# Regrouping gate jobs, gate loads and one mix in a hybrid trunk step on one core

## The chip, the cores and the metric

The kernel runs on one core of one Trainium2 chip. The metric is the time of one execution on the device in microseconds (us); for a kernel it is the median of its runs.

## The reference

The program is one inference step of a trunk with two layers (`DEPTH = 2`) on 384 tokens of width 1024: 128 context tokens and 256 tokens of a denoising step. A layer mixes tokens in four parallel branches, which share one input projection, and then applies a mixture of 16 experts. The gates of the branches come from the same projection; the change touches their computation and the differential attention.

```python
h = rms_norm(x, p['norm1_w']) * (1 + scale1) + shift1
(mq, mk, mv, mo, mg, nq, nk, nv, dq, dk, dv, sz, sxbc, sdt, gpre) = split_cols(h @ p['w_in'])
...
br = jnp.stack([a_out, b_out, c_out, d_out], axis=2)
gates = jax.nn.sigmoid(gpre.reshape(B, S, N_BRANCH, D_MODEL))
mixed = jnp.sum(gates * jnp.einsum('bsnc,ncd->bsnd', br, p['w_branch']), axis=2)
x = x + gate1 * (mixed @ p['w_out'])
h2 = rms_norm(x, p['norm2_w']) * (1 + scale2) + shift2
x = x + gate2 * expert_choice_ffn(h2, p['w_router'], p['w_gate'], p['w_up'], p['w_down'])
```

The branches are an mLSTM and an SSD scan (each in both directions), a neighbourhood attention and a differential attention, where `a = p[0] - lam * p[1]` mixes two softmaxes before the product with the values.

## The kernel before

Each engine has its own instruction list, written out by hand, and the lists meet by semaphores. In a layer's mixing stage TensorE does, in this order: the input projection (L887 to L905), the neighbourhood attention (L1001), the differential attention (L1062), the scans (L1104 to L1191), a tail of jobs (L1193), the transposes of the branch outputs (L1200), the branch products (L1209), the output products (L1223). Then comes the expert stage (L1246 to L1409), whose weights are streamed from HBM into seven slots.

**Jobs.** The 4096 gate columns of `w_in` are cut into 32 gate jobs (`g0` to `g31`), 24 matmuls of 128x384 each: three passes of split weights over eight blocks of rows. Eight parts (`p`) and sums (`s`) of the modulation weights `w_ada` make 16 more. Their order is the table `JOB_SITES` (L118): every entry is a place in TensorE's list where `job()` (L916) is called, with the jobs done there. ScalarE takes each job's bank in the same order with `take_job()` (L1553): two banks serve in turn, so a job waits until the job two before it is taken. Gates 0 to 23 are stored to HBM as they are taken (L1571; the issue comes with the next take); gates 24 to 31 stay in `GATES`.

**Splits.** Before a quarter of a weight tile is used, ScalarE copies its rounded part into one of four buffers (`high_parts`, L1470) and GpSimd subtracts it (`low_parts`, L709, L717). `AHEAD` (L243) says up to which quarter ScalarE splits after each job; a quarter can be split when its tile has landed and the job four before it is done. `high_parts` waits for the landing of a tile when it comes to the tile's first quarter. The branch weights are two tiles of 2 MB and their first quarter waits for both (L548).

**Loads.** SyncE issues the tile loads in the order of `JOB_TILES` (L139, loop L635), each after the job that frees its slot: a tile of gates after the last gate of the tile two before, an ada tile after the part before. Then it issues the two branch tiles (L645), waiting first for gate 27 and then for part 7, and after all jobs the saved x and the first half of `w_out` (L648 to L650).

**Differential attention.** VectorE finds the maxima of a unit (`df_max`), mixes the two softmaxes (`df_mix`, L2054) and takes the product of an earlier unit out of its bank (`df_take`, L2064). The loop is at L2069. TensorE's `df_turn(u)` (L1042) waits for mix u, `df_out(u)` (L1052) for the take of unit u-1.

**Scans.** For each of the two scans VectorE turns eight decay rows into exponents, and multiplies them with TensorE's scores (`decays`, L2088). TensorE does four jobs among the first rows, one behind the last rows, two behind the last scores (L1126, L1127), two ahead of the state products (L1144), and in the second scan one, two and three (L1160 to L1171). ScalarE's takes are placed to match (L1643 to L1666).

**From the tail to the branch products.** VectorE's norms end with `br_ready` (L2234). TensorE waits for it, transposes the outputs into six banks and does the last job. ScalarE copies the six banks (L1667), takes the last job, and issues the first four gate loads (L1674 to L1681): 576 KB each, two of them into the room of the scan's work tiles once `br_ready` is there, two into room that VectorE's `tokens_free` (L2254) gives free. VectorE makes the low part of each bank behind ScalarE's copy (L2245), then waits for the stores of the states and sets `tokens_free`. Each branch product (eight, L1209) is 24 matmuls; VectorE gates it (L2256 to L2267) with a loaded gate tile; the third product and each later one waits for the gating of the one two before.

Of the kernel before, what the change touches and what calls it, by code (L numbers as in the profile page):

```python
# [70 lines left out]
def constants():  # L71
# [31 lines left out]
    for g in range(4):  # L103
        for r in range(2):
# [19 lines left out]
JOB_ORDER = tuple(_s[1] for _s in JOB_SITES)  # L124
NA_JOBS = [len(_s[1].split()) for _s in JOB_SITES if _s[0] == "na"]
DF_JOBS = [len(_s[1].split()) for _s in JOB_SITES if _s[0] == "df"]
# [120 lines left out]
SPILLED = 24  # L247
# [16 lines left out]
def trunk_program(nc, dr, outs):  # L264

    (y_prompt, y_sample, new_na_k, new_na_v, new_diff_k, new_diff_v, new_C, new_n, new_m, new_ssm) = outs
    with ExitStack() as ctx:
# [3 lines left out]
        sem = {n: ctx.enter_context(nc.semaphore(n)) for n in SEMS}  # L271
# [5 lines left out]
        spilled = [ctx.enter_context(nc.semaphore(f"spilled{i}")) for i in range(8)]  # L277
# [16 lines left out]
        def rounded(v):  # L294
            return bass.AP(as_fp32r[v.tensor.name], v.offset, v.ap)
# [469 lines left out]
        def _(pe):  # L765
# [62 lines left out]
            for l in range(L):  # L828
# [87 lines left out]
                def job():  # L916

                    j = jobs[0]
                    jobs[0] += 1
                    kind, i = JOBS[j]  # L920
                    if j >= 2:
                        pe.wait_ge(sem["job_evac"], NJ * l + j - 1)
                    else:
                        pe.wait_ge(sem["proj_evac"], N_PROJ * l + (19, N_PROJ)[j])
                    if kind == "sum":
                        pe.wait_ge(sem["job_evac"], NJ * l + JOBS.index(("part", i)) + 1)
                        mm = ada_sum(job_bank(j), MPL(i))
                    elif kind == "part":
                        mm = ada_partial(job_bank(j), tile(("mix", l, 7 + [t_[:2] for t_ in JOB_TILES].index(("ada", i)))))
                    else:  # L930
                        hi, lo_ = next_quarter()[0]
                        for k in range(KC):
                            mm = three_passes(PS[:, job_bank(j), 0:T], (hi[:, k, :], lo_[:, k, :]), h_in(k), k == 0, k == KC - 1)
                    mm.then_inc(sem["job_out"], 1)
# [189 lines left out]
                pe.wait_ge(sem["pm_ready"], 16 * l + 6)  # L1124
                scores(0, 3)
                job()  # L1126
                job()  # L1127

                pe.wait_ge(sem["pm_ready"], 16 * l + 8)
                for i, (t, d, b, bq) in enumerate(((0, 0, 2, None), (0, 1, 3, None), (1, 0, 4, 5), (1, 1, 6, 7), (2, 0, 2, 3), (2, 1, 4, 5))):  # L1130
# [30 lines left out]
                decay_row(1, 4)  # L1161
                decay_row(1, 5)
                job()
                job()
                decay_row(1, 6)
                decay_row(1, 7)
                pe.wait_ge(sem["pm_ready"], 16 * l + 12)
# [22 lines left out]
                        mm = pe.matmul(PS[0:64, 5, 64 * c:64 * c + 64], KW[:, d, h, :], BTM[:, 64 * (h // 2):64 * (h // 2) + 64], start=True, stop=True)  # L1190
                mm.then_inc(sem["st_out"], 1)  # L1191

                for _ in range(6):  # L1193
                    job()


# [222 lines left out]
        def _(act):  # L1419
            def copy(dst, src, scale=1.0):  # L1420
                return act.activation(dst, src, ACT.Copy, scale=scale)  # L1421
# [45 lines left out]
            for l in range(L):  # L1467
# [175 lines left out]
                for c in range(8):  # L1643
                    decayed(0, c)
                    if c >= 2:
                        take_job()
                take_job()

                act.activation(W1[:, 0:768].rearrange("p (a b) -> p a b", a=TT), MO[:, :, :], ACT.Tanh, scale=0.5)
                act.activation(W1[:, 768:1536].rearrange("p (a b) -> p a b", a=TT), SZ[:, :, :], ACT.Tanh, scale=0.5).then_inc(sem["tanh_out"], 1)  # L1650
# [4 lines left out]
                    copy(CN_OUT[0:64, d, :, :], PS[0:64, 7 if d == 0 else 2, 0:260].rearrange("p (a b) -> p a b", a=4)).then_inc(sem["st_evac"], 1)  # L1655
                for c in range(8):
                    decayed(1, c)
                    if 2 <= c <= 4:
                        take_job()
                take_job()  # L1660
                take_job()
                take_job()
                act.wait_ge(sem["st_out"], 2 * l + 2)
                copy(SS_OUT[0:64, :, :], PS[0:64, 5, :].rearrange("p (a b) -> p a b", a=8)).then_inc(sem["st_evac"], 1)
                for _ in range(6):
                    take_job()  # L1666
                for g in range(6):  # L1667
                    t, half = g // 2, g % 2
                    act.wait_ge(sem["brt_out"], 6 * l + g + 1)
                    copy(rounded(BRT[:, 4 * half:4 * half + 4, t * 128:(t + 1) * 128]), PS[:, 2 + g, :].rearrange("p (a b) -> p a b", a=4)).then_inc(sem["brt_evac"], 1)  # L1670
                take_job()


                for slot in spilled:  # L1674
                    act.wait_ge(slot, 16 * (SPILLED // 8) * (l + 1))
                for dc in range(4):
                    if dc == 0:
                        act.wait_ge(sem["br_ready"], l + 1)
                    if dc == 2:
                        act.wait_ge(sem["tokens_free"], l + 1)  # L1680
                    act.dma_start(GT[dc % 4], spill[l, dc]).then_inc(gate_in[dc % 4], 16)  # L1681
                for dc in range(8):
                    high_parts(Q_BRANCH + dc + 5)
                    act.wait_ge(sem["bp_evac"], 8 * l + dc + 1)
# [91 lines left out]
        def _(dve):  # L1776
# [34 lines left out]
            for l in range(L):  # L1811
# [233 lines left out]
                def df_max(u):  # L2045
                    dve.wait_ge(sem["ds_out"], 12 * l + u + 1)
                    if u >= 2:
                        dve.wait_ge(sem["dpt_out"], 12 * l + u - 1)
                    i, w = u % 2, (128 if u < 4 else 384)
                    dve.tensor_reduce(SMX[:, i, :], PS[:, 2 + 2 * i:4 + 2 * i, 0:w], AX.X, ALU.max, negate=True).then_inc(dve_step, 1)  # L2050
                    dve.wait_ge(dve_step, step())
                    TS(DMX[:, i, :], SMX[:, i, :], 32 ** -0.5, None, ALU.mult).then_inc(sem["d_max"], 1)
# [13 lines left out]
                    t, h = u // 4, u % 4  # L2066
                    dve.tensor_copy(DQK[:, t, h * 64:h * 64 + 64], PS[:, 7, 0:64]).then_inc(sem["do_evac"], 1)

                for i in range(15):  # L2069
                    if i < 12:  # L2070
                        df_max(i)
                    if i >= 3:
                        df_take(i - 3)
                    if 1 <= i <= 12:
                        df_mix(i - 1)

                def head_norm(src, n, c, scale, eps, power, lo):

# [326 lines left out]
```

## Time and profile before

| | |
|---|---|
| median of 3 runs | 1991.64 us (1990.75 to 1997.35) |
| the profiled execution's own time | 1997.49 us |
| its span in the profile | 1995.7 us |
| TensorE matmuls busy | 1786.2 us (90%) |
| VectorE busy | 632.3 us (32%) |
| ScalarE busy | 556.9 us (28%) |
| GpSimd busy | 513.6 us (26%) |
| mean granted clock of TensorE | 0.98 |
| DMA | 567.78 MB, mean 285 GB/s |

PE is TensorE, PEld its weight loads, DVE VectorE, ACT ScalarE, POOL GpSimd, SP SyncE; a q behind a name is that engine's DMA issue. A time is counted from the start of the span. Busy time says how long an engine had instructions running; the chain of the profile says which of them set the end. Layer 0's mixing stage lies at about 60 to 500 us and layer 1's at 1035 to 1480 us; the expert stages, with the DMA engines nearly full, lie behind each.

### The profile page before, as it was taken

The page shows a single profiled execution, that of the slowest core. Times are in us where ns is not written, and L with a number is a line of the kernel's source. Part 1 is how long each engine was busy: PE and PEld are TensorE (multiplying, and loading weights), DVE is VectorE, ACT ScalarE, POOL GpSimd, SP SyncE. Part 2 cuts the span into 40 slices and gives each one's busy share as a digit, 9 for nine tenths or more (in the row PEclk, how much of TensorE's full clock was granted, in tenths as well). Part 3 has the DMA queues.
Part 4 walks back from the last instruction along what each step waited for, and adds up shares of the span by engine and source line. Part 5 has one row for each costly group of instructions (what it writes and reads, how often), then busy time and mean ns, then how long its engine had stood idle before and what let it go on. Part 6 is the DMA issues. An engine that isn't in the chain of part 4 may idle for free.

```text
span 1995.7 us, 22783 instructions
## 1 busy us (share of the span) xinstructions
PE 1786.2 (90%) x9208; PEld 1138.6 (57%) x9208; DVE 632.3 (32%) x1363; ACT 556.9 (28%) x1070; POOL 513.6 (26%) x654
## 2 busy tenths in 40 slices
PE   6999999979899888888889999998999988888787
PEld 3788997879443222222258889887975322222223
DVE  1287344764400000101144853548622000000011
ACT  3444344223421101111144444432333111011011
POOL 0787344246100000000037754424631000000000
PEclk8999999989999999999999999899999999999999
DMA  9535534465799999999973354353465999999996
GB/s 349 126 104 182 192 117 156 130 231 193 297 376 426 427 425 428 427 427 427 426 211 127 106 204 154 109 189 132 169 253 211 404 428 426 426 428 427 427 426 260
DMA packets 123544, 567.78 MB, mean 285 GB/s; under 512 B 21808, under 2 KB 31280, under 8 KB 98352
## 3 DMA queue, kind: packets, MB, share of 16 engines
q1 hardware_dynamic: 112656, 543.91, 68.9%
q10 hardware_dynamic: 9920, 20.84, 2.8%
q0 software_dynamic: 864, 1.58, 0.3%
q8 instruction: 73, 1.20, 0.2%
q14 instruction: 31, 0.25, 0.0%
HBM read 550.57 MB, written 15.73 MB: 284 GB/s over the span
## 4 chain that ended last, share of the span: by engine, by line
PE 54%; DMA 36%; DVE 6%; ACT 2%; SPq 1%; issue 1%; POOL 0%; ACTq 0%; DVEq 0%
PE banks L776 29%; PE banks L1322 11%; DMA work<-in_w_gate 7%; DMA ring<-in_w_up 6%; DMA work<-in_w_up 6%; DMA ring<-in_w_down 6%; DMA ring<-in_w_gate 4%; DMA work<-in_w_down 3%; PE banks L782 2%; DMA ring<-in_w_ada 1%; PE banks L1082 1%; PE banks L1292 1%; PE banks L788 1%; ACT work L1421 1%; DMA work<-gates_spill 1%; ACT hT L1450 1%
## 5 line engine op out<-in xcount | busy, mean ns | idle before, releaser
L717 POOL TENSOR_TENSOR ring_fp32r<-ring,ring_fp32r 128x256 fp32r<-128x256 f32 x592 | 461.3, 812 | 854.9 <-ACT ring_fp32r L1421 854.2
L1322 PE MATMUL banks<-ring,work 128*64 128x512 f32 x1776 | 402.7, 597 | 77.0 <-DMA ring<-in_w_gate 33.5
L776 PE MATMUL banks<-xT_fp32r,ring_fp32r 128*128 128x384 f32 x1280 | 349.9, 346 | 1.8 <-POOL ring_fp32r L717 1.8
L1421 ACT ACTIVATE work<-banks 32x512 f32<-32x512 f32 (+7 forms) x404 | 205.4, 529 | 454.4 <-PE banks L1322 250.8
L1322 PEld LDWEIGHTS banks<-ring,work 128*64 128x64 f32 x1776 | 122.5, 136 | 335.4 <-issue 199.0
L1322 PE MATMUL banks<-work 128*64 128x512 f32 x972 | 225.8, 601 | 40.4 <-DMA work<-in_w_gate 14.9
L776 PEld LDWEIGHTS banks<-xT_fp32r,ring_fp32r 128*128 128x128 f32 x1280 | 237.2, 191 | 14.7 <-issue 7.2
L776 PE MATMUL banks<-hT_fp32r,ring_fp32r 128*128 128x384 f32 x640 | 217.3, 340 | 0.0
L2317 DVE SCALAR_TENSOR_TENSOR xT<-banks,mod,xT 128x128 f32<-128x128 f32 (+1 forms) x128 | 47.1, 413 | 445.5 <-PE banks L1358 445.1
L1421 ACT ACTIVATE ring_fp32r<-ring 128x1024 fp32r<-128x1024 f32 (+1 forms) x164 | 154.5, 969 | 94.1 <-PE banks L776 74.2
L1322 PEld LDWEIGHTS banks<-work 128*64 128x64 f32 x972 | 67.5, 137 | 180.7 <-issue 112.5
L1727 ACT ACTIVATE work<-banks 128x512 f32<-128x512 f32 x32 | 19.1, 597 | 483.5 <-PE banks L1322 483.5
L776 PE MATMUL banks<-work_fp32r,ring_fp32r 128*128 128x384 f32 x768 | 142.7, 346 | 8.3 <-DVE work L2267 8.3
L776 PEld LDWEIGHTS banks<-work_fp32r,ring_fp32r 128*128 128x128 f32 x768 | 137.5, 192 | 11.6 <-DVE work L2267 8.9
L776 PE MATMUL banks<-ring_fp32r,xT_fp32r 128*128 128x512 f32 (+1 forms) x480 | 136.2, 369 | 1.2 <-DVE small L1857 1.2
L776 PEld LDWEIGHTS banks<-hT_fp32r,ring_fp32r 128*128 128x128 f32 x640 | 122.6, 192 | 1.3 <-issue 0.3
L2339 DVE TENSOR_TENSOR work<-work,banks 128x512 f32<-128x512 f32 x32 | 22.0, 688 | 292.3 <-PE banks L1322 292.2
L776 PEld LDWEIGHTS banks<-ring_fp32r,xT_fp32r 128*128 128x128 f32 x480 | 86.7, 189 | 16.1 <-DVE small L1857 1.4
L1322 PE MATMUL banks<-hT,work 128*64 128x512 f32 x324 | 75.2, 599 | 20.7 <-DMA work<-in_w_gate 8.2
L776 PE MATMUL banks<-ring_fp32r,hT_fp32r 128*128 128x512 f32 (+1 forms) x240 | 88.4, 368 | 0.0
L1566 ACT ACTIVATE work<-banks 128x384 f32<-128x384 f32 x64 | 31.3, 489 | 163.0 <-PE banks L776 163.0
L2336 DVE SCALAR_TENSOR_TENSOR work<-work,banks 128x512 f32<-128x512 f32 x32 | 21.8, 681 | 124.8 <-ACT work L1421 67.9
(293 smaller groups left out, 1736.1 us busy)
## 6 DMA issues: line engine op xcount, KB each, us to landing
ring<-in_w_up SPq DMA_DIRECT2D x38, 2048.0 KB, 30.6
ring<-in_w_gate SPq DMA_DIRECT2D x37, 2048.0 KB, 30.6
ring<-in_w_down SPq DMA_DIRECT2D x36, 2048.0 KB, 30.1
ring<-in_w_in SPq DMA_DIRECT2D x28, 2048.0 KB, 8.3
ring<-in_w_ada SPq DMA_DIRECT2D x24, 2048.0 KB, 8.4
work<-in_w_down SPq DMA_DIRECT2D x20, 2048.0 KB, 30.6
work<-in_w_gate SPq DMA_DIRECT2D x18, 2048.0 KB, 30.6
work<-in_w_up SPq DMA_DIRECT2D x16, 2048.0 KB, 30.6
```

Of the source, the lines that this page charges most:

```text
L717: ins = pool.tensor_tensor(rounded(w_), w_, rounded(hi_), ALU.subtract)
L776: mm = pe.matmul(dst, a_, b_, start=(first and i == 0), stop=(last and i == 2))
L782: mm = pe.matmul(PS[32 * g:32 * g + 32, bank, :], c32[:, k, :], w[:, k, :], start=(k < 4), stop=(k >= 4), tile_position=(0, 32 * g))
L788: mm = pe.matmul(PS[:, bank, 2 * j:2 * j + 2], partial[:, j // 2, 128 * (j % 2):128 * (j % 2) + 128], K("adasel"), start=True, stop=True)
L1082: pe.matmul(PS[:, 4 + c % 4, 0:T], ident[:, r:r + 1].broadcast_to([128, 128]), ROWS[:, 0, :], start=True, stop=True)\
L1292: mm = pe.matmul(dst, rounded(strided(part[:, t, 512 * (q // 8):512 * (q // 8) + 512], q // 2 % 4)), rounded(SEL[:, t, a:b, :].rearrange(" ...
L1322: mm = pe.matmul(dst[64 * hf:64 * hf + 64, :], x(k), w[kk][:, 512 * hf:512 * hf + 512], start=(k == 0), stop=(k == KC - 1), tile_position= ...
L1421: return act.activation(dst, src, ACT.Copy, scale=scale)
L1566: ins = act.activation(GATES[:, i % 8, :], PS[:, job_bank(j), 0:T], ACT.Tanh, scale=0.5)
L2317: ins = STT(xT[:, dc, a:b], PS[:, bank, a:b], mod[:, 40 + dc, g:g + 1], xT[:, dc, a:b], ALU.mult, ALU.add)
L2336: STT(SA, TH, 1.0, PS[:, 2 * (e % 2), :], ALU.add, ALU.mult).then_inc(dve_step, 1)
L2339: TTo(HH[:, e % 2, :], SA, PS[:, 2 * (e % 2) + 1, :], ALU.mult).then_inc(sem["hh_ready"], 1)
```

## The change

Gate 23 and those behind it move later in the job order: the scans have two gate jobs less and the tail has eight jobs in place of six, with part 7 ahead of gate 27. ScalarE's takes follow. ScalarE issues the first two gate loads ahead of its copies of the branch banks and the next two ahead of its take of the last job. VectorE does the last differential mix ahead of the takes of units 9, 10 and 11.

```diff
-             ("scan0", "g20"), ("scan0", "p3"), ("scan0", "g21 s3"), ("scan0", "g22"), ("scan0", "p4 g23"),
-             ("state0", "s4 p5"), ("scan1", "g24"), ("scan1", "s5 g25"), ("state1", "p6 g26 s6"), ("tail", "g27 p7 g28 s7 g29 g30"), ("branch", "g31"))
+             ("scan0", "g20"), ("scan0", "p3"), ("scan0", "g21 s3"), ("scan0", "g22"), ("scan0", "p4"),
+             ("state0", "s4 p5"), ("scan1", "g23"), ("scan1", "s5"), ("state1", "p6 g24 s6"), ("tail", "g25 p7 g26 s7 g27 g28 g29 g30"), ("branch", "g31"))
...
                 scores(0, 3)
                 job()
-                job()
...
                 decay_row(1, 5)
                 job()
-                job()
                 decay_row(1, 6)
...
-                for _ in range(6):
+                for _ in range(8):
                     job()
...
                     if c >= 2:
                         take_job()
-                take_job()
...
-                    if 2 <= c <= 4:
+                    if 2 <= c <= 3:
                         take_job()
...
-                for _ in range(6):
+                for _ in range(8):
                     take_job()
+                for slot in spilled:
+                    act.wait_ge(slot, 16 * (SPILLED // 8) * (l + 1))
+                act.wait_ge(sem["br_ready"], l + 1)
+                for dc in range(2):
+                    act.dma_start(GT[dc], spill[l, dc]).then_inc(gate_in[dc], 16)
                 for g in range(6):
                     t, half = g // 2, g % 2
                     act.wait_ge(sem["brt_out"], 6 * l + g + 1)
                     copy(rounded(BRT[:, 4 * half:4 * half + 4, t * 128:(t + 1) * 128]), PS[:, 2 + g, :].rearrange("p (a b) -> p a b", a=4)).then_inc(sem["brt_evac"], 1)
+                act.wait_ge(sem["tokens_free"], l + 1)
+                for dc in range(2, 4):
+                    act.dma_start(GT[dc], spill[l, dc]).then_inc(gate_in[dc], 16)
                 take_job()
-                for slot in spilled:
-                    act.wait_ge(slot, 16 * (SPILLED // 8) * (l + 1))
-                for dc in range(4):
-                    if dc == 0:
-                        act.wait_ge(sem["br_ready"], l + 1)
-                    if dc == 2:
-                        act.wait_ge(sem["tokens_free"], l + 1)
-                    act.dma_start(GT[dc % 4], spill[l, dc]).then_inc(gate_in[dc % 4], 16)
...
-                for i in range(15):
-                    if i < 12:
-                        df_max(i)
+                for i in range(12):
+                    df_max(i)
                     if i >= 3:
                         df_take(i - 3)
-                    if 1 <= i <= 12:
+                    if i >= 1:
                         df_mix(i - 1)
+                df_mix(11)
+                for i in range(9, 12):
+                    df_take(i)
```

## Rows read from the trace of the kernel before

**Rows 1.** The page's costliest groups of instructions.

```profile
L1322 PE MATMUL banks<-ring,work 128*64 128x512 f32 x1776 | 402.7, 597 | 77.0 <-DMA ring<-in_w_gate 33.5
```

**Rows 2.** Chain that ended last, in order of time, layer 0.

```profile
340.83 4.36 PE banks L776 x24
...
368.56 4.30 PE banks L776 x24
372.86 1.29 PE banks L1082 x4
...
415.57 1.38 DVE work L2234
...
427.12 9.20 DMA work<-gates_spill
```

**Rows 3.** TensorE in order of time: start us, us, what [idle before <-releaser].

```profile
308.90 0.55 PE L1049 MATMUL banks<-cst,work 128*128 128x128 f32 x3 [2.15 <-DVE work L2062]
...
391.71 0.44 PE L776 MATMUL banks<-xT_fp32r,ring_fp32r 128*128 128x384 f32 x1
...
416.99 5.38 PE L1204 MATMUL banks<-cst,work 128*128 128x128 f32 x24 [5.38 <-DVE work L2234]
...
440.03 39.53 PE L776 MATMUL banks<-work_fp32r,ring_fp32r 128*128 128x384 f32 x216 [4.82 <-DVE work L2267]
...
1284.64 0.55 PE L1049 MATMUL banks<-cst,work 128*128 128x128 f32 x3 [2.16 <-DVE work L2062]
...
1370.48 0.44 PE L776 MATMUL banks<-xT_fp32r,ring_fp32r 128*128 128x384 f32 x1
...
1397.65 5.13 PE L1204 MATMUL banks<-cst,work 128*128 128x128 f32 x24 [7.27 <-DVE work L2234]
...
1418.88 21.33 PE L776 MATMUL banks<-work_fp32r,ring_fp32r 128*128 128x384 f32 x111 [3.47 <-DVE work L2267]
...
1509.70 0.36 PE L1272 MATMUL banks<-cst,work 16*128 16x16 f32 x3 [1.10 <-DVE work L2304]
```

**Rows 4.** VectorE in order of time, layer 0.

```profile
304.47 1.06 DVE L2062 SCALAR_TENSOR_TENSOR work<-work,small 128x384 f32<-128x384 f32 x1
...
340.20 0.42 DVE L2120 TENSOR_TENSOR work<-work,banks 128x256 f32<-128x256 f32 x1
...
368.91 0.41 DVE L2120 TENSOR_TENSOR work<-work,banks 128x256 f32<-128x256 f32 x1
...
384.08 1.37 DVE L2178 TENSOR_TENSOR work<-work 128x768 f32<-128x768 f32 x1
...
409.23 0.96 DVE L2229 TENSOR_TENSOR work<-work 128x768 f32<-128x768 f32 x1
```

**Rows 5.** Stretches: us, busy PE PEld DVE ACT POOL, granted clock, DMA, GB/s.

```profile
308.90:321.18 12.28, 11.96 (x57) 8.92 (x61) 5.71 (x20) 2.39 (x4) 4.63 (x7) 0.86 0.39 150
1284.64:1299.95 15.31, 14.99 (x57) 11.16 (x61) 5.71 (x20) 2.38 (x4) 4.62 (x7) 0.67 0.32 123
...
1509.70:1515.00 5.30, 5.20 (x21) 2.85 (x21) 4.00 (x7) 1.06 (x2) 0.00 (x0) 1.00 0.00 0
```

**Rows 6.** SyncE's queue in order of time, both layers.

```profile
396.18 2.25 SPq L563 DMA_DIRECT2D ring<-in_w_branch  x2
...
1374.94 2.25 SPq L563 DMA_DIRECT2D ring<-in_w_branch  x2
```

**Rows 7.** ScalarE in order of time, both layers.

```profile
414.15 2.19 ACT L1421 ACTIVATE ring_fp32r<-ring 128x512 fp32r<-128x512 f32 x4 [6.17 <-DMA ring<-in_w_branch]
...
416.61 1.14 ACT L1421 ACTIVATE ring_fp32r<-ring 128x512 fp32r<-128x512 f32 x2
...
1391.38 2.19 ACT L1421 ACTIVATE ring_fp32r<-ring 128x512 fp32r<-128x512 f32 x4 [4.64 <-DMA ring<-in_w_branch]
...
1402.22 1.20 ACT L1421 ACTIVATE work_fp32r<-banks 128x512 fp32r<-128x512 f32 x2 [0.26 <-PE banks L1204]
```

**Rows 8.** Line 563, the weight loads of 320 to 420 us.

```profile
DMA to landing us min/median/max: 7.7/9.7/16.0
```

## The prediction

> **What bounds the kernel now.** First I read, among the page's costliest groups, the expert matmuls (L1322): of the 77.0 us that TensorE stood idle before one group of them, a load of gate weights ended the largest part, 33.5 [rows 1]. The expert stages are a stream of weight loads, set off by the branch and output products at the end of each mixing stage; so a microsecond saved before that end should move the rest of the program one for one.
>
> Then I read the chain that ended last, in order of time, through layer 0's mixing stage [rows 2]. Two gate jobs lie on it inside the scans (4.36 and 4.30 us). Behind the scans it is one VectorE chain, the norms that end with br_ready at 415.57 + 1.38 = 416.95; then TensorE transposes the branches, does the last gate job, and the first branch product waits for a 9.20 us gate load before the stream of 216 matmuls starts at 440.03.
>
> Last I read TensorE's own order of time with its waits in brackets [rows 3]. TensorE is without a gap from 308.90 to the end of the tail jobs (416.99 - 5.38 = 411.61). Its waits in layer 0 are 2.15 (last differential mix), 5.38 (br_ready) and 4.82 us (gate load); in layer 1 they are 2.16, 7.27 and 3.47. That is all this change can win by filling gaps, except what the clock gives back.
>
> **The mix ahead of three takes.** VectorE ended the mix before the last at 304.47 + 1.06 = 305.53 [rows 4], and stood until TensorE came to 308.90 - 2.15 = 306.75, because a take that needs TensorE's product was ahead of the last mix; take (some 0.2) and mix then filled TensorE's wait of 2.15 [rows 3]. Without the take ahead the mix starts at 305.53 and costs 1.95 (its length as it was) to 2.8 us (GpSimd splits beside it until then, and a VectorE product is 1.37 us beside a split for 0.96 without [rows 4]). It ends at 307.5 to 308.3, and TensorE waits 0.7 to 1.6 in place of 2.15: I take 1.1, so 1.05 saved per layer. The three takes behind it come up to 1 us later, under the transposes of the last unit.
>
> **The clock behind that wait.** From the end of the wait to the end of the first scan job layer 0 takes 12.28 us at a granted clock of 0.86, layer 1 15.31 us at 0.67 [rows 5]: part of it runs at 1.2 GHz and the rest at 2.4. All at 2.4 GHz it would be about 10.5 (busy time times granted clock, plus the 0.32 idle), so 1.8 and 4.8 us hang on the clock. A wait of 1.10 elsewhere was followed by a granted clock of 1.00 [rows 3, 5], and 1.1 is what I expect here; but that is one row, in a stretch of other work. The ends are 0 and 6.6 us, and I take half, 3.3.
>
> **Two jobs out of the scans.** 4.36 + 4.30 = 8.66 us leave TensorE's gapless stretch. What would be late next is VectorE: the score products behind the first job wait for its last decay product, which ended at 340.20 + 0.42 = 340.62 against 340.83 when the removed job began, and those behind the second for 368.91 + 0.41 = 369.32 against 368.56 + 1.29 (the decay rows that stood behind the job, at 372.86) = 369.85 [rows 2, 4]. Both are just in time, so the whole 8.66 counts. The bounds are 0 (VectorE slips by as much) and 8.66.
>
> So the first tail job starts 8.66 + 1.05 = 9.7 earlier, at 382.0 for 391.71, and in layer 1 at 1360.8 for 1370.48. I count on from that start, s.
>
> **The tail.** It took 411.61 - 391.71 = 19.9 us; with two more jobs it takes 28.5. br_ready came at s + 25.2 (layer 0) and s + 27.1 (layer 1, 1397.65). GpSimd's splits now fall more into the VectorE chain. By the 0.41 that a 768-column product loses, and about three such steps under a split, two more splits in layer 0 cost some 2 us and one more in layer 1 some 1. br_ready thus comes at s + 27 to 28, hidden by the jobs. The wait for it is gone.
>
> **What is late next: the branch weights.** Their two 2 MB loads are issued in order by SyncE, the first after gate 27. That job was the first of the tail (ending at s + 4.4); now two gates, part 7 and sum 7 stand before it. Four gates, the part and the sum made the 19.9, so part and sum are 19.9 - 4 x 4.33 = 2.6, and it ends at 3 x 4.36 + 2.6 = s + 15.7; part 7's load stands behind its own. In layer 0 the first load was issued at 396.18 and ScalarE went on with the split of both at 414.15, 17.97 later; in layer 1 it was 1374.94 and 1391.38, 16.44 later [rows 6, 7]. I take the middle, 17.2: landing at s + 33 (15.8 with the issue). ScalarE waits for it right behind its take of gate 28, and behind that wait stand, in its order: the takes of gates 29 and 30, three splits, the first two gate loads, and the six copies of the turned branches. From 414.15 to the end of the third split (416.61 + 1.14) took 3.6; with both takes 4.1. The copies run 0.60 each [rows 7], 3.5 together, and VectorE's last low part ends 0.7 later. So TensorE, which has turned the branches by s + 28.5 + 5.4 = 33.9, starts the products at 33.0 + 4.1 + 3.5 + 0.7 = s + 41.3. The last gate job lies inside that stretch (it needs gate 29's take at s + 34.5).
>
> The Trainium skill, DMA: Bandwidth & Descriptors, sections Bandwidth and Latency and other measured facts, gives 425 GB/s for a large read and about 2 us of fixed cost. By that, as an estimate, 4.2 MB land 11.9 us after the issue, 5.3 sooner, and the program would take 1961. The two measured landings disagree with it, and the sum goes by them.
>
> **Gate loads ahead of the last job.** Their issue moves from 427.12 to behind br_ready and the third split, s + 37. With the 9.20 us of the row [rows 2], where two more of them were beside them, they would land at s + 46.2, and probably sooner. The first product ends at 41.3 + 4.2 = s + 45.5. So the wait shrinks to 0 to 0.7; the second product (to s + 49.7) covers VectorE's 3.6 us of gating, and the long stream starts at s + 49.7. The other two loads now wait for tokens_free ahead of the last take; that take then comes at s + 42, and TensorE wants it for the second product at s + 45.5. The waits for the spill stores are over long before (gate 23's store moves with its job and is still issued ahead of the tail). The wait for br_ready ahead of the copies costs nothing, as the transposes need it anyway.
>
> **Moved past.** On SyncE the tile of gates 28 to 31 is loaded after gate 23, behind the sixth ada tile: issued about 362, landing some 10 later, split at 373. Ada tile 5 now has 10 us instead of 14 until its job; 7.7 us was the quickest load of this stretch [rows 8], so a wait of up to 1 us is possible. GpSimd's state stores go out behind the splits of gates 29 and 31, by s + 22, some 20 ahead of tokens_free, which waits for them.
>
> **Sum.** The long stream started at 440.03 - 391.71 = s + 48.3 and at 1418.88 - 1370.48 = s + 48.4. Now it is s + 49.7 with s 9.7 earlier: 8.4 saved per layer, 16.8 in both, and 3.3 from the clock: 20.1 us. The profiled execution's own time is 1997.49 (span 1995.70), 5.9 above the median of the three runs and at their upper end; the change comes off either. Against 1991.64 that is 1971.5.
>
> **Rivals.**
> - *The branch weights are not late.* A 2 MB load by itself lands in 7.7 us [rows 8], two of them side by side thus in 7.7 to 15.4, by the middle 11.6 in place of 17.2: landing at s + 27.4, products start at s + 35.7, the gate load (s + 31.5 + 9.2) and VectorE's 3.6 put the stream at s + 44.3, 13.7 saved per layer. 1991.6 - 27.4 - 3.3 = **1961**. Against it stand both measured pairs; for it, that no other load now runs beside them.
> - *The weights come later by some microseconds*, or the idle time that is left brings 1.2 GHz into the products: 4 to 7 per layer, **1978 to 1985**.
> - *The scans do not get shorter.* The two margins are 0.21 and 0.53 us; if VectorE slips, the jobs move but nothing ends sooner: s + 49.7 against s + 48.3 with s 1.05 earlier, 0.3 lost per layer, less the clock's 3.3: **1989**, no change.
> - *Slower: the two loads land one behind the other.* If each takes the longest landing measured, 16.0 [rows 8], the second lands 32 after the issue, 14.8 later than I count: 6.4 lost per layer, 12.8 less 3.3, **2001**. It decides from a landing 25.6 us after the issue on. Against it: the pair took 16.4 and 18.0 though issued 1.9 apart.
>
> **How the numbers follow.** A measurement of this kernel can tell 0.3%, 6 us, from no change. Forecast 0.58 (its own range 1966 to 1978), weights early 0.17, weights later 0.10, scans unchanged 0.08, loads in series 0.07. The first three are faster: 0.85; same 0.08; slower 0.07. The range from 1960 to 1984 leaves out the last two and the outer ends of the second and third, 0.2 in all.
>
> **What would show it.** TensorE's wait ahead of the last differential transposes near 1 us; no job between the last decay row's scores and the numerators; the tail gapless for 28.5 us and the branch transposes without a wait; a ScalarE wait of some 12 us for in_w_branch behind gate 28; a wait of 2 to 5 us around the last gate job; no wait of VectorE for gates_spill over 1 us. I am wrong if the scans keep their length, if that ScalarE wait is gone, or if the expert stages stretch by what the mixing stages save.

## The result and the profile after

The changed kernel took 1971.29 us in the median of 4 runs (1969.93 to 1972.82) beside 1991.2 for the kernel before (4 runs): a ratio of 0.9902, 95% interval 0.9878 to 0.9926. The forecast was 1971.5. The profiled execution took 1972.1 us (span 1970.3, clock 0.988). Lines of the changed kernel stand one to three numbers lower than before (L1204 is now L1202, L1421 is L1419, L2062 is L2059), and one higher again where the stores are moved. Here and below, "1.33 for 2.15" means 1.33 where it was 2.15.

TensorE in order of time, with the waits in brackets, first layer 0 and then layer 1:

```profile
305.89 0.55 PE L1049 MATMUL banks<-cst,work 128*128 128x128 f32 x3 [1.33 <-DVE work L2059]
...
407.15 2.84 PE L1202 MATMUL banks<-cst,work 128*128 128x128 f32 x24 [0.22 <-DVE work L2233]
414.73 0.69 PE L776 MATMUL banks<-xT_fp32r,ring_fp32r 128*128 128x384 f32 x1 [4.75 <-ACT work L1564]
...
1270.73 0.55 PE L1049 MATMUL banks<-cst,work 128*128 128x128 f32 x3 [1.33 <-DVE work L2059]
...
1371.99 2.84 PE L1202 MATMUL banks<-cst,work 128*128 128x128 f32 x24 [0.22 <-DVE work L2233]
1379.66 0.45 PE L776 MATMUL banks<-xT_fp32r,ring_fp32r 128*128 128x384 f32 x1 [4.83 <-ACT work L1564]
1386.43 1.82 PE L776 MATMUL banks<-work_fp32r,ring_fp32r 128*128 128x384 f32 x9 [0.74 <-issue]
```

Beside [rows 3]: the wait for the last mix is 1.33 for 2.15; that for br_ready is 0.22 for 5.38 and 7.27; the gate-load wait (4.82 and 3.47) is gone. A new wait stands ahead of the last gate job, 4.75 and 4.83 us, put down to ScalarE's take.

The chain that ended last, in order of time, says what that take waited for:

```profile
334.33 1.85 PE banks L782 x16
336.18 2.82 PE banks L1098 x24
...
358.96 0.79 PE banks L788 x8
359.75 1.40 PE banks L1082 x4
...
378.77 4.37 PE banks L776 x24
383.14 1.85 PE banks L782 x16
...
394.89 18.20 DMA ring<-in_w_branch
414.73 53.49 PE banks L776 x288
...
1379.66 6.03 PE banks L776 x24
...
1386.43 46.51 PE banks L776 x264
```

In the scans the numerators (L1098) and the second direction's scores (L1082) now stand right behind an ada job (a part, L782, or a sum, L788); the two gate jobs that [rows 2] had there are gone. The tail starts at 378.77 for 391.71. What the last gate job waited for, by this chain, is the load of the branch weights, 18.20 us on it. ScalarE and SyncE in order of time agree:

```profile
394.47 4.00 SPq L563 DMA_DIRECT2D ring<-in_w_branch  x2
...
413.15 1.15 ACT L1419 ACTIVATE ring_fp32r<-ring 128x512 fp32r<-128x512 f32 x2 [14.02 <-DMA ring<-in_w_branch]
413.80 0.81 ACTq L1668 DMA_DIRECT2D work<-gates_spill  x2
...
417.03 3.02 ACT L1419 ACTIVATE work_fp32r<-banks 128x512 fp32r<-128x512 f32 x6
```

From the issue to the split of the weights it is 413.15 - 394.47 = 18.68 us. ScalarE stood 14.02 of them, with the takes of gates 29 and 30 behind it, and TensorE needs the first of these for its last gate job.

The stretches of [rows 5], of the same lengths from the end of the mix wait:

```profile
305.89:318.17 12.28, 11.96 (x69) 8.56 (x69) 5.79 (x21) 3.90 (x7) 5.32 (x8) 1.00 0.50 191
1270.73:1286.04 15.31, 14.99 (x81) 10.53 (x82) 7.11 (x26) 4.50 (x8) 5.31 (x8) 1.00 0.51 174
```

The granted clock behind the mix wait is 1.00 in both layers, for 0.86 and 0.67, and the same time holds 69 and 81 matmuls (the first count in brackets) for 57 and 57. The expert stream, in the page's costliest groups, has not changed, so what the mixing stages save the program saves:

```profile
L1320 PE MATMUL banks<-ring,work 128*64 128x512 f32 x1776 | 404.4, 599 | 77.9 <-DMA ring<-in_w_gate 33.3
```

**Where the time came from.** From the start of the mix wait (before 308.90 - 2.15, after 305.89 - 1.33) to the end of the branch products (before 440.03 + 39.53 by [rows 3], after 414.73 + 53.49) layer 0 takes 163.66 us for 172.81: 9.15 saved. In layer 1 the same stretch ends at 1386.43 + 46.51 for 1418.88 + 39.65 = 1458.53 and takes 163.54 for 176.05: 12.5 saved. The row of before:

```profile
1418.88 39.65 PE L776 MATMUL banks<-work_fp32r,ring_fp32r 128*128 128x384 f32 x216 [3.47 <-DVE work L2267]
```

Together 21.7; the medians differ by 19.9. The spans of the two profiled executions differ by more, 25.4 us: 2.2 of these lie ahead of the first mix wait and 1.7 between the two stretches, where the change moves nothing; they are not counted as its gain.

### The profile page after: what moved, and what is told of

Same layout as the page of the kernel before. It is cut to its first block, busy times and chain, and to the rows that moved or that the text cites. A ratio compares the mean times of both kernels' runs of the same rounds, so it can differ in the third digit from the quotient of the medians.

```text
span 1970.3 us, 22783 instructions
## 1 busy us (share of the span) xinstructions
PE 1772.6 (90%) x9208; PEld 1128.7 (57%) x9208; DVE 634.2 (32%) x1363; ACT 555.9 (28%) x1070; POOL 514.5 (26%) x654
## 4 chain that ended last, share of the span: by engine, by line
PE 56%; DMA 37%; DVE 3%; ACT 2%; SPq 1%; issue 0%; POOL 0%; ACTq 0%; DVEq 0%
PE banks L776 31%; PE banks L1320 11%; DMA work<-in_w_gate 7%; DMA work<-in_w_up 6%; DMA ring<-in_w_down 6%; DMA ring<-in_w_up 6%; DMA ring<-in_w_gate 4%; DMA work<-in_w_down 3%; PE banks L782 2%; DMA ring<-in_w_branch 2%; PE banks L1098 1%; DMA ring<-in_w_ada 1%; PE banks L1082 1%; PE banks L1290 1%; PE banks L788 1%; ACT work L1419 1%
## 5 line engine op out<-in xcount | busy, mean ns | idle before, releaser
L1419 ACT ACTIVATE work<-banks 32x512 f32<-32x512 f32 (+7 forms) x404 | 205.4, 529 | 452.4 <-PE banks L1320 253.1
L1419 ACT ACTIVATE ring_fp32r<-ring 128x1024 fp32r<-128x1024 f32 (+1 forms) x164 | 154.8, 970 | 106.9 <-PE banks L776 69.5
```

## The experiments

The theory after this reading: the three parts add up, and what the two moved jobs save in the scans is mostly eaten by the branch weights. The rival: those weights are late for a reason that an earlier issue does not change. The kernels ran in three groups, each beside its own runs of the kernel before (medians 1991.72 of 17 runs, 1995.42 of 6, 1992.79 of 10).

| kernel | median us | ratio to before | 95% interval |
|---|---|---|---|
| mix_only | 1983.06 | 0.9963 | 0.9949 to 0.9977 |
| loads_only | 1982.62 | 0.9953 | 0.9938 to 0.9969 |
| jobs_only | 1988.88 | 0.9984 | 0.9969 to 0.9999 |
| branch_split | 1958.64 | 0.9833 | 0.9818 to 0.9849 |
| branch_late | 1972.03 | 0.9883 | 0.9865 to 0.9901 |
| mix_loads | 1970.51 | 0.9876 | 0.9859 to 0.9894 |
| branch_split_p7 | 1955.11 | 0.9802 | 0.9782 to 0.9821 |
| branch_best | 1959.63 | 0.9819 | 0.9803 to 0.9835 |
| stores_early | 1965.68 | 0.9866 | 0.9841 to 0.9890 |
| p7_stores_early | 1955.28 | 0.9807 | 0.9787 to 0.9827 |
| mix_loads_stores | 1977.98 | 0.9921 | 0.9899 to 0.9942 |
| after_again | 1971.31 | 0.9890 | 0.9872 to 0.9908 |

### The three parts, each alone

**mix_only**: the kernel before with this part of the change.

```diff
-                for i in range(15):
-                    if i < 12:
-                        df_max(i)
+                for i in range(12):
+                    df_max(i)
...
+                df_mix(11)
+                for i in range(9, 12):
+                    df_take(i)
```

> Against the kernel before at 1991.2. Theory (each part is worth the TensorE wait that it closes, and the waits do not overlap): the wait ahead of the last differential transposes falls from 2.15 to 1.33 us as in the changed kernel, 1.6 us in both layers, and up to 6.6 more if the clock stays at 2.4 GHz behind it: 1983 to 1990. Rival (the mix only shifts a wait to the take behind it): 1991, with a new wait of TensorE ahead of the last unit's product.

1983.06, as expected. The two waits are 1.34 and 1.33 and the clock behind both is 1.00. The gain, 0.37% or 7.4 us (4.6 to 10.2 by its interval), is far more than the 0.82 saved per layer; the stretches of 12 to 15 us behind this wait, over all kernels of this study, put the rest down to the clock. With a wait of 2.14 or 2.15 (before, loads_only, jobs_only) the granted clock was 0.86, 0.67, 1.00, 0.67, 0.86 and 1.00; with 1.33 or 1.34 it was 1.00 in 21 of 22 (0.86 in layer 0 of branch_best).

**loads_only**: the kernel before with ScalarE's gate loads moved as in the change.

```diff
+                act.wait_ge(sem["br_ready"], l + 1)
+                for dc in range(2):
+                    act.dma_start(GT[dc], spill[l, dc]).then_inc(gate_in[dc], 16)
                 for g in range(6):
...
+                act.wait_ge(sem["tokens_free"], l + 1)
+                for dc in range(2, 4):
+                    act.dma_start(GT[dc], spill[l, dc]).then_inc(gate_in[dc], 16)
                 take_job()
```

> Against the kernel before at 1991.2. Theory: the gate loads, issued at br_ready some 9 us sooner, land before the first product ends; the waits of 4.82 and 3.47 us ahead of the third product go: 8.3 us, with up to 3 more from the clock behind them: 1980 to 1983. Rival (the loads only come into the way of the saved x and the output weights, or the take of the last job behind tokens_free is the new wait): 1989 to 1993.

1982.62, as expected. In its chain of waits the transposes still wait for br_ready (6.38 and 6.41 in TensorE's order of time), but the last gate job and all products then run without a gap:

```profile
417.64 4.91 PE banks L1204 x24
422.55 50.46 PE banks L776 x288
```

The gain, 0.47% or 9.4 us (6.2 to 12.3 by its interval), agrees with the two waits (4.82 + 3.47) and some clock behind them. Before, the 216 matmuls behind the wait took 39.53 us [rows 3]; in the changed kernel 264 take 46.51 in layer 1, so 216 would take 38.05. The wait thus had a clock price of some 1.5 us per layer behind it; the granted clock of the first 6 us behind it was 0.73 and 0.72.

**jobs_only**: the kernel before with the new `JOB_SITES`, the `job()` calls and the takes of the change.

```diff
-("scan0", "p4 g23"), ("state0", "s4 p5"), ("scan1", "g24"), ("scan1", "s5 g25"),
+("scan0", "p4"), ("state0", "s4 p5"), ("scan1", "g23"), ("scan1", "s5"),
...
-                for _ in range(6):
+                for _ in range(8):
                     job()
```

> Against the kernel before at 1991.2. Theory: the tail starts 8.7 us sooner, but the branch weights land 18.7 after gate 27 and the gate loads are issued only after the last job, so the third product starts at s + 53 in place of s + 48.3: 3.7 us saved per layer, 1984. Rival (the moved jobs are nearly the whole gain of the change): 17 us, 1974.

1988.88, a smaller gain than expected. The wait for br_ready is gone (0.23), but TensorE waits for the branch weights instead, and the gate-load wait stays:

```profile
420.23 0.69 PE L776 MATMUL banks<-xT_fp32r,ring_fp32r 128*128 128x384 f32 x1 [5.25 <-ACT work L1564]
...
440.56 9.69 PE L776 MATMUL banks<-work_fp32r,ring_fp32r 128*128 128x384 f32 x46 [4.61 <-DVE work L2264]
```

So 8.66 us leave the scans of each layer and 1.6 us of the program's time per layer are left, by an interval that nearly reaches no change. The three gains add to 1.00%, and the change has 0.98%. That the parts add up does not follow from it: mix_loads, below, breaks it.

### Are the branch weights what takes the jobs' gain?

**branch_split**: the changed kernel; SyncE loads part 7's half of the branch weights first, and no longer behind gate 27.

```diff
-for i, job in enumerate((("gate", 27), ("part", 7))):
+for i, job in ((1, ("part", 7)), (0, ("gate", 27))):
```

> The changed kernel (1971.3), with SyncE waiting for part 7 and loading its half of the branch weights first, then gate 27 and the other half. Theory (ScalarE's wait of 14.0 us for the branch weights is what holds the last gate job, TensorE's waits of 4.75 and 4.83): only one tile is left to land behind gate 27, some 8 to 11 us after it in place of 18.7, so TensorE's wait goes and the products start 4 to 5 us sooner in each layer: 1961 to 1963. Rival (the wait is hidden by the copies of the branch banks and the gate loads behind it): 1970 to 1972.

1958.64, better than expected and 12.7 below the change. The first half goes out at 386.90, and ScalarE's split, which needs both, comes at 408.99 for 413.15. The wait ahead of the last gate job is gone in both layers; what is left stands ahead of the products:

```profile
417.34 32.98 PE L776 MATMUL banks<-work_fp32r,ring_fp32r 128*128 128x384 f32 x186 [1.33 <-issue]
...
1375.69 46.52 PE L776 MATMUL banks<-work_fp32r,ring_fp32r 128*128 128x384 f32 x264 [1.00 <-issue]
```

**mix_loads**: the kernel before with both other parts, without the moved jobs (the diffs of mix_only and loads_only).

> The kernel before with the mix and the gate loads of the change, and its own job order. If the parts add up, 0.9963 x 0.9953 = 0.9916 of the kernel before, 1975, and the moved jobs are worth only some 3 to 4 us in the changed kernel. Rival (the jobs make room for the loads, so the parts need each other): 1980 or more.

1970.51: faster than both expectations, and as fast as the whole change (1971.29, and 1971.31 in the repeat; branch_late, in the same group, 1972.03). The two parts together gain 1.24% where alone they gain 0.84% in sum; the kernel before ran 3.7 us slower in this group than in the first, and how much of the difference is real stays open. The sum of three that matched the change was thus a coincidence. The transposes of mix_loads wait 5.39 and 7.29 us for br_ready, and nothing waits behind. From the start of the mix wait to the end of the branch products it takes 163.60 and 164.34 us, the change 163.66 and 163.54. So in the change as it stands the moved jobs are worth nothing that these runs can tell: they exchange the wait for br_ready for the one on the weights. Either has 1.2 GHz behind it for a part: the granted clock is 0.72 in the change's last gate job of layer 1, which takes 6.03 us (the tail's first 4.37), and 0.52 in the transposes of mix_loads in layer 0. The change first, then mix_loads:

```profile
1379.66:1385.69 6.03, 6.03 (x24) 5.71 (x24) 3.04 (x6) 5.32 (x11) 6.03 (x10) 0.72 0.59 196
```

```profile
414.23:419.57 5.34, 5.34 (x25) 5.34 (x26) 4.79 (x9) 3.57 (x7) 5.34 (x9) 0.52 0.60 221
```

**branch_late**: the changed kernel; the first branch load waits for gate 28 and not for gate 27.

```diff
-for i, job in enumerate((("gate", 27), ("part", 7))):
+for i, job in enumerate((("gate", 28), ("part", 7))):
```

> The changed kernel (1971.3) with the first branch load waiting for gate 28 in place of gate 27, so both land one gate job (4.4 us) later. Theory (that landing holds ScalarE, and behind it TensorE): 4.4 us more in each layer, TensorE's wait ahead of the last gate job 9.1 for 4.75: 1980. Rival (the landing has slack behind it): 1971 to 1973.

1972.03: nothing lost. The loads go out 3.6 us later and the weights are there no later:

```profile
398.10 0.92 SPq L563 DMA_DIRECT2D ring<-in_w_branch  x2
...
412.81 1.15 ACT L1419 ACTIVATE ring_fp32r<-ring 128x512 fp32r<-128x512 f32 x2 [14.21 <-DMA ring<-in_w_branch]
```

412.81 - 398.10 = 14.7 us for 18.68. My theory that the landing counts from the issue fell. Something else let the load go, at the same moment in both kernels.

### What holds the load

In the kernel before, the change, mix_only, loads_only, jobs_only, mix_loads and branch_late the branch load is issued behind GpSimd's stores of the states (new_C and new_n). In all of them, in both layers, it came to full rate (over 380 GB/s, in stretches of 1 us) 11 to 12.5 us after the issue of the last of these stores, whenever it was itself issued. In the changed kernel that store goes out at 390.49:

```profile
390.49 0.63 POOL L744 DMA_DIRECT2D out<-work  x1
```

The stretches of 2 us from there (last two columns: DMA share and GB/s) show the load issued at 394.47 hardly moving until 402:

```profile
394.00:396.00 2.00, 2.00 (x13) 2.00 (x12) 1.90 (x7) 1.44 (x2) 0.00 (x1) 1.00 2.01 35
396.00:398.00 2.00, 2.00 (x14) 2.00 (x13) 1.90 (x6) 0.00 (x0) 2.00 (x3) 1.00 0.33 4
398.00:400.00 2.00, 2.00 (x13) 2.00 (x12) 1.93 (x3) 0.49 (x1) 2.00 (x3) 1.00 0.42 20
400.00:402.00 2.00, 2.00 (x13) 2.00 (x13) 1.93 (x3) 0.00 (x0) 0.61 (x1) 1.00 0.42 88
402.00:404.00 2.00, 2.00 (x14) 2.00 (x13) 1.76 (x8) 0.00 (x0) 0.00 (x0) 1.00 0.99 406
```

**stores_early**: the changed kernel with these stores ahead of the later splits.

```diff
                 low_parts(AHEAD[29])
-                low_parts(AHEAD[39])
+                low_parts(AHEAD[33])
                 pool.wait_ge(sem["st_evac"], 3 * l + 2)
...
+                low_parts(AHEAD[39])
                 low_parts(Q_BRANCH)
```

> The changed kernel with GpSimd's four state stores of a layer (new_C and new_n) moved ahead of the split of the weights for the last gate jobs, so that they are issued some 30 us before the branch loads and not 4 us before gate 27's half. Theory A (the stores hold the branch load: in every kernel so far it flowed at full rate only some 10 to 12 us after the last of these stores was issued): the load flows at once, lands 11 to 13 us after its issue and not 18.7, TensorE's waits of 4.75 and 4.83 us ahead of the last gate job go, and the time is 1961 to 1964 us beside some 1971 for the changed kernel. Rival B (the trickle at the start is the load's own, or comes from the gate spills or the gate weights' loads): landing 18 to 19 us, waits and time unchanged, 1971 us.

1965.68, a little over the expected 1961 to 1964 and 5.6 below the repeat of the change on the same chip (after_again): the intervals of the two ratios overlap, but five of the six runs lie below all six of the repeat. The last store is out at 352.17, the branch loads go out at 394.47 as before, and they flow:

```profile
352.17 0.63 POOL L744 DMA_DIRECT2D out<-work  x1
```

```profile
394.00:396.00 2.00, 2.00 (x13) 2.00 (x12) 1.88 (x7) 1.44 (x2) 0.29 (x2) 1.00 0.22 20
396.00:398.00 2.00, 2.00 (x13) 2.00 (x13) 1.95 (x2) 0.00 (x0) 2.00 (x2) 1.00 0.85 313
398.00:400.00 2.00, 2.00 (x14) 2.00 (x12) 1.97 (x2) 0.50 (x1) 2.00 (x3) 1.00 1.00 406
```

```profile
408.70 1.15 ACT L1420 ACTIVATE ring_fp32r<-ring 128x512 fp32r<-128x512 f32 x2 [9.57 <-DMA ring<-in_w_branch]
...
410.28 0.45 PE L777 MATMUL banks<-xT_fp32r,ring_fp32r 128*128 128x384 f32 x1 [0.74 <-ACT work L1565]
417.06 1.30 PE L777 MATMUL banks<-work_fp32r,ring_fp32r 128*128 128x384 f32 x4 [2.32 <-issue]
```

Full rate from 397 on and not from 402, the weights at 408.70 for 413.15, and TensorE's wait ahead of the last gate job 0.74 for 4.75. That the stores hold the load is shown; the rival, a start that is the load's own or comes from the gate spills or gate loads, which are all still there, is out. Two sizes were off. The landing took 14.2 us and not 11 to 13, and more than half of the 4.0 us gained there goes to a new wait of 2.32 us: behind the weights ScalarE still does three splits, two takes and six copies, 8.36 us until the products. What in the stores holds it, the 64 KB of new_C or the 4-byte elements of new_n, was not taken apart.

The stores did not become harmless by the move: they now hold the loads that follow them at the new place. The tile of gates 28 to 31 is issued at 357.70 both here and in the change, and here it lands 13.9 us later for 10.5. Its rate over 4 us, first here, then in the change:

```profile
360.00:364.00 4.00, 4.00 (x26) 1.69 (x24) 2.87 (x10) 1.26 (x2) 2.01 (x3) 1.00 0.53 55
```

```profile
360.00:364.00 4.00, 4.00 (x26) 1.69 (x24) 2.87 (x10) 1.26 (x2) 2.01 (x3) 1.00 1.00 343
```

It comes to full rate at 365, 12.8 us after the last store. The ada tile issued at 348.2, just ahead of the stores, lands after 13.3 us for 7.6; in layer 1 TensorE waits 0.46 us for it, and 0.45 and 1.16 us in p7_stores_early, where the change has no such wait. It also says more of branch_split: its first half was issued 3.5 us ahead of the stores and landed after 7.7 us, the second behind them after 12.6.

**mix_loads_stores**: mix_loads with the same move of the stores.

> The kernel before with the mix reordered, the gate loads early and the state stores ahead, but its own job order (two gate jobs stay in the scans). If the moved jobs lost their gain only because the branch weights came late, then here, where TensorE waits for the branch transposes (br_ready, 5.4 and 7.3 us) and not for the weights, the early stores give nothing: 1969 to 1972 us, and the distance to stores_early, 7 to 10 us, is what the moved jobs are worth once the weights are there. Rival (the moved jobs are worth nothing in any case): both kernels come out within 2 us of one another.

1977.98: both expectations missed, it is 7.5 slower than mix_loads (0.45%, some 9 us, by the ratios, as the two ran in different groups). The weights come sooner here too (14.3 us after the issue for 17.8), and that is the harm: GpSimd's split of them now runs beside the small VectorE operations ahead of br_ready. GpSimd, VectorE and TensorE in order of time:

```profile
409.28 6.19 POOL L717 TENSOR_TENSOR ring_fp32r<-ring,ring_fp32r 128x256 fp32r<-128x256 f32 x9 [9.41 <-ACT ring_fp32r L1422]
...
412.11 0.65 DVE L1797 TENSOR_TENSOR work<-work,small 128x3 f32<-128x3 f32 x1
...
419.57 4.34 PE L1205 MATMUL banks<-cst,work 128*128 128x128 f32 x24 [10.38 <-DVE work L2237]
```

In mix_loads, where GpSimd stood still until 412.44, the same operation took:

```profile
411.43 0.16 DVE L1796 TENSOR_TENSOR work<-work,small 128x3 f32<-128x3 f32 x1
```

Eleven such operations at 0.65 for 0.16 are 5.4 us, and br_ready's wait is 10.38 for 5.39. In layer 1 it is 10.13 for 7.29; there the last three of these operations ran beside the split in mix_loads already. With the jobs moved (stores_early) br_ready is over by 405.8 and the split starts at 409.9: no collision. So with the weights in time the two kernels lie 1977.98 - 1965.68 = 12.3 us apart, and with late weights they are equal. But most of the 12.3 is the harm that the earlier split does without the moved jobs. Against mix_loads, the better kernel without them, stores_early is 4.8 faster by the medians and 0.1% by the ratios, which noise allows to be nothing. What is shown is that the same move of the stores gains 5.6 us with the moved jobs and costs 7.5 without them. branch_split without the moved jobs was not run.

### The fastest version

**branch_split_p7**: branch_split with part 7 ahead of the tail's gates, so that its half of the weights can be issued at once.

```diff
-("tail", "g25 p7 g26 s7 g27 g28 g29 g30")
+("tail", "p7 g25 g26 g27 s7 g28 g29 g30")
```

> The kernel with the branch loads in turn (1958.6), and the tail in the order part 7, gates 25, 26, 27, sum 7, 28, 29, 30: one half of the branch weights is loaded from the first tail job on, gate 27 ends 0.8 sooner. Theory (one tile's landing still ends 1.3 and 1.0 us of TensorE's waits): 1 to 2 us less, 1957. Rival (TensorE and VectorE now meet at br_ready, and nothing is left): 1958 to 1959.

1955.11 (1952.88 to 1960.88), where 1957 was expected: the lowest median here, 16 us below the change. What part 7 adds to branch_split is not settled, as their intervals touch. In the chain of waits the whole tail, the transposes and the products are one piece without a gap:

```profile
381.80 1.85 PE banks L782 x16
383.65 12.68 PE banks L776 x72
396.33 0.79 PE banks L788 x8
397.12 12.62 PE banks L776 x72
409.74 2.62 PE banks L1202 x24
412.36 50.44 PE banks L776 x288
```

**branch_best**: branch_split_p7 with ScalarE's splits of the branch weights only behind gate 30's take, so that no take waits behind them.

```diff
-free = q < Q_BRANCH + 4 and j >= JOBS.index(("part", 7)) + 3
+free = q < Q_BRANCH + 4 and j >= JOBS.index(("gate", 30))
```

> As the kernel with part 7 first in the tail, and the splits of the branch weights only from the take of gate 30 on, so that two splits in place of three stand ahead of the copies of the branch banks. Theory (the copies end 1.1 us sooner and TensorE's last wait ahead of the products goes): 1956. Rival: as with part 7 first alone.

1959.63, where 1956 was expected: no gain, the interval overlaps with that of branch_split_p7. There was no wait left to remove.

**p7_stores_early**: branch_split_p7 with the stores ahead.

> The fastest kernel so far (branch_split_p7: part 7 first in the tail, its half of the branch weights loaded first) with the state stores ahead as well. There TensorE has no wait left in the tail, so theory A expects earlier landings of both branch halves, but no time: 1954 to 1957 us, as without it. Rival: the third weight split and the rounding copies start earlier and the product stream gains 1 to 3 us more, or a load that is no longer held collides with the gate spills and costs as much.

1955.28, as fast as without: where TensorE does not wait for the weights, their earlier landing is worth nothing.

**after_again**: the changed kernel, unaltered, as the level for this group.

> The changed kernel once more, beside the three others on the same chip: 1970 to 1973 us, ratio 0.988 to 0.992 to the kernel before. It is the level from which the early stores are counted in this call.

1971.31, as expected.

## Why the prediction was right

The mechanism held, and the sum to 0.2 us, which is in part luck: without the clock the stretches above save 7.5 us per layer and not 8.4, 1.8 less in both, and the clock gave more than the 3.3 counted; the two errors pull against each other. The terms, one by one:

- *The mix, 1.05 per layer.* Measured 0.82 (2.15 to 1.33): the wait stayed nearer to the upper end.
- *The clock, half of 6.6.* All of it came in the profiled execution: 1.00 in both layers. But the wait of 2.15 brings the lower clock in four of six stretches only, so what the change takes away differs from one execution of the kernel before to the next. The ends 0 and 6.6 were right. By the clocks of the six stretches the mean price is some 2.2 us per layer, 4.4 in both, so half was 1.1 short.
- *8.66 out of the scans.* Held: from the start of the mix wait to the tail's start layer 0 takes 74.21 us for 84.96, 10.75 less, of which 0.82 is the mix and some 1.7 the clock (12.28 at 0.86 for 1.00). The rest, 8.2, falls 0.4 short of 8.66, so VectorE's narrow margins held.
- *br_ready hidden.* Right, with nothing to spare: TensorE's tail ended at s + 28.2 and then waited 0.22 for br_ready, which came at s + 28.3, forecast at s + 27 to 28.
- *The weights, 17.2 after the issue.* Right in kind, 18.68 and 18.77 in size: s + 34.4 for s + 33. The 4.75 wait around the last gate job is the one named. The reason was not in the prediction. It took the landing for a property of the loads, and a good part of it, 4.5 us by stores_early, is one of what GpSimd stores ahead of them. The Trainium skill, DMA: Bandwidth & Descriptors, sections Bandwidth and Latency and other measured facts, gives 425 GB/s for a large read and some 2 us of fixed cost, by which, as an estimate, the pair lands after 11.9 us. The rate agrees once the load flows (406 to 422 GB/s), the start does not.
- *4.1 + 3.5 + 0.7 from there to the products.* Measured 421.78 - 413.15 = 8.63 for 8.3. The copies took 0.50 each and not 0.60; the rest went to VectorE's 3.68 behind them. The last gate job, which was to lie inside the stretch for nothing, ran at 1.2 GHz for a part (granted clock 0.57, and 0.72 in layer 1) and ended where the products began (0.74 ahead in layer 1).
- *The gate loads.* No wait was left, where 0 to 0.7 was forecast.
- *The long stream at s + 49.7, 1.4 later than before.* Layer 0's products end 89.45 after s for 87.85 before: 1.6 later.

Among the rivals, "the weights are not late" asked for a landing of 11.6; the quickest pair issued together landed in 13.97 (stores_early, layer 1). "In series" was out as well. What the prediction did not price is what the moved jobs bring by themselves: 8.66 less in the scans, 8.66 more in the tail, and a wait of 5 to 7 us for br_ready exchanged for one of nearly 5 on the weights. The 20 us come from the mix, the gate loads and the clock behind both; mix_loads is as fast without the jobs.

## What to carry to other kernels

When a step is moved off the chain, ask what ends the next wait, and test the parts alone: a part that looks like the largest can be worth nothing as long as the next thing is late, and still decide whether an earlier load pays (5.6 us won with it, 7.5 lost without). Parts that add up alone need not add up in pairs. Where a load lands later than its bytes explain, look in the DMA rates for the moment at which it starts to flow, and at what other queues were given just before. And an earlier load is not free: look what the work that it lets go runs beside. Nor is a store that was moved out of the way: look which load it stands ahead of now.

## What the runs showed of the hardware that was not expected

- State stores issued on GpSimd's queue held a 4 MB load on SyncE's queue to a trickle (4 to 88 GB/s) until 11 to 13 us after the last of them was issued; with the stores moved away (stores_early) it flowed 2.5 us after its issue, and a gate load behind their new place was held in the same way (55 GB/s for 343).
- VectorE operations on 128x3 elements took 0.65 us beside a GpSimd subtraction (mix_loads_stores) and 0.16 without (mix_loads): four times, where 128x768 products take 1.37 for 0.96 [rows 4].
- Behind a TensorE wait of 2.15 us the granted clock fell in four stretches of six, behind 1.33 or 1.34 in one of 22.
